# Hybrid attention trunk on one core: value products five steps behind the scores, inverse sums of two heads turned together

## The reference, cut to what matters

```python
logits = jnp.einsum('bqhd,bkhd->bhqk', qb, k, preferred_element_type=jnp.float32) * scale
...
p = jax.nn.softmax(logits, axis=-1)
return jnp.einsum('bhqk,bkhd->bqhd', p.astype(v.dtype), v)
```

## Time and profile before

| | us |
|---|---|
| median of 3 runs | 3393.14 (3392.2 to 3406.85) |
| profiled execution, its own time | 3396.07 |
| its span | 3394.3 |
| PE, DVE, ACT, POOL busy | 3024.3, 1362.0, 880.8, 936.2 |
| granted clock of TensorE, mean | 0.94 |
| even attention | 290 to 684 |
| odd attention | 1963 to 2459: small kinds to 2283, then sel and win |

### The profile page before, as it was taken

The page is one execution under the profiler, slowest core; times in us unless marked ns, Lnnn a source line. Parts: engine busy times, 40 slices in busy tenths (PEclk is TensorE's granted clock), DMA queues, the critical chain, the costliest instruction groups (busy, mean ns, idle before and its releaser), DMA issues.

```text
span 3394.3 us, 38000 instructions
## 1 busy us (share of the span) xinstructions
PE 3024.3 (89%) x14116; PEld 2484.8 (73%) x14116; DVE 1362.0 (40%) x1945; ACT 880.8 (26%) x1593; POOL 936.2 (28%) x562
## 2 busy tenths in 40 slices
PE   8896778798999999999999966767689999999999
PEld 5775777775888888876788855656667888888867
DVE  4634666606222222227523246576534222222264
ACT  2204555513011011024200044545531111111131
POOL 2330033242233233252233202121132333333342
PEclk9998999999999999999999965769889999999999
DMA  4236321120111111111235252434311111111102
GB/s 158 107 118 174 94 72 42 32 99 25 50 50 43 49 49 43 50 58 43 80 148 195 78 142 71 97 79 102 87 58 44 47 47 49 45 48 49 61 33 75
DMA packets 73794, 253.72 MB, mean 75 GB/s; under 512 B 9699, under 2 KB 13283, under 8 KB 73367
## 3 DMA queue, kind: packets, MB, share of 16 engines
q1 hardware_dynamic: 58728, 196.35, 19.5%
q10 hardware_dynamic: 14944, 55.74, 4.2%
HBM read 203.99 MB, written 52.78 MB: 76 GB/s over the span
## 4 chain that ended last, share of the span: by engine, by line
PE 75%; DVE 15%; issue 4%; ACT 3%; DMA 1%; POOL 0%; SPq 0%; DVEq 0%; ACTq 0%; POOLq 0%
PE ACC L1033 59%; PE OP L1196 5%; PE ACC L1165 3%; PE OP L1212 3%; DVE PT L1791 3%; PE TR L1179 2%; DVE R L1641 2%; DVE T L1664 1%; DVE H L1667 1%; PE OP L1089 1%; DVE XL L1647 1%; ACT PT L1437 1%; DVE XF L1832 1%; DVE T L1689 1%; DVE HL L1692 1%
## 5 line engine op out<-in xcount | busy, mean ns | idle before, releaser
L863 POOL CAST WH<-RAW 128x1024 fp32r<-128x1024 f32 x203 | 216.3, 1066 | 1577.8 <-PE ACC L1033 1558.0
L1033 PE MATMUL ACC<-XH,WH 128*128 128x512 f32 x1792 | 575.4, 402 | 70.5 <-DVE XL L1647 39.0
L1033 PE MATMUL ACC<-XL,WH 128*128 128x512 f32 x1792 | 556.7, 392 | 0.0
L1033 PE MATMUL ACC<-XH,WL 128*128 128x512 f32 x1792 | 555.7, 391 | 0.0
L865 POOL TENSOR_TENSOR WL<-RAW,WH 128x1024 fp32r<-128x1024 f32 x203 | 495.6, 2442 | 24.2
L1033 PEld LDWEIGHTS ACC<-XH,WH 128*128 128x128 f32 x1792 | 337.6, 190 | 171.3 <-issue 87.7
L1033 PEld LDWEIGHTS ACC<-XL,WH 128*128 128x128 f32 x1792 | 339.3, 189 | 71.8
L1033 PEld LDWEIGHTS ACC<-XH,WL 128*128 128x128 f32 x1792 | 339.0, 189 | 71.9
L1394 ACT ACTIVATE HH<-T 128x1024 fp32r<-128x1024 f32 x64 | 67.9, 1061 | 1168.4 <-DVE T L1689 1168.4
L1696 DVE TENSOR_TENSOR M<-M,ACC 128x1024 f32<-128x1024 f32 x128 | 156.3, 1221 | 495.8 <-PE ACC L1033 495.8
L1033 PE MATMUL ACC<-HH,WH 128*128 128x512 f32 x1024 | 316.7, 390 | 17.0 <-DVE HL L1692 17.0
(11 more groups left out here) (193 smaller groups left out, 3636.7 us busy)
## 6 DMA issues: line engine op xcount, KB each, us to landing
RAW<-in_w SPq DMA_DIRECT2D x203, 512.0 KB, 3.4
QK<-y_odds SPq DMA_DIRECT2D x128, 256.0 KB, 5.0
y_odds<-HALVES ACTq DMA_DIRECT2D x16, 1024.0 KB, 5.0
QK<-y_foxs SPq DMA_DIRECT2D x48, 256.0 KB, 5.4
y_foxs<-HALVES ACTq DMA_DIRECT2D x8, 1024.0 KB, 5.1
y_kv<-Q ACTq DMA_DIRECT2D x8, 512.0 KB, 2.6
BIAS<-y_f SPq DMA_DIRECT2D x8, 512.0 KB, 7.0
H<-in_xT ACTq DMA_DIRECT2D x8, 512.0 KB, 6.9
```

Source lines behind the costliest of these rows:

```text
L863: nc.gpsimd.tensor_copy(WH[:, slot], RAW[:, slot]).then_inc(s_whi, 1)
L1033: mm = nc.tensor.matmul(acc[:, h * HALF:(h + 1) * HALF], w(k), x[:, k, h * HALF:(h + 1) * HALF], start=first and k == k0 and w is ws and x ...
```

## The change

`VALUE_LAG` goes from 3 to 5, and PE issues `values` ahead of `turn` in a step. The outputs follow at lag 6 in place of 4. PB has four buffers for large kinds in place of three, and OP's two banks alternate by half.

`norm` goes. For halves of head e = 1 alone POOL's `spread` lays the inverse sums of both heads, 64 columns a head, over a SPREAD buffer (in dilated jobs the sums into one, the minima into the other); three steps later PE's `turn_spread` turns its four blocks into the next TR buffer, and one step after that DVE multiplies the 128 rows of both heads in one instruction (in dilated jobs ACT copies the sums, DVE the minima, 128 rows each). That group's TR buffer is free at `s_fin` (sums: `s_dl`). The halves of the mla heads are split in eight pieces of 512 columns over steps 0 to 5. RV, SPREAD and PB have other places in memory.

```diff
-TURN_LAG, VALUE_LAG = 2, 3
+TURN_LAG, VALUE_LAG = 2, 5
+SPLIT_STEPS = {0: (0, 1), 1: (2,), 2: (3,), 3: (4, 5), 4: (6,), 5: (7,)}
...
-        depth = 8 if t.small else 3
+        depth = 8 if t.small else 4
...
+            if st.norm and st.norm.e == 1:
+                st.norm.groups = [group(0, 4, st.norm, what)
+                                  for what in (("sums", "minima") if st.norm.job.kind in DILATED else ("inverse",))]
...
             if g.seq > 2:
                 x = pt_groups[g.seq - 3]
-                if x.kind == "A":
-                    eng.wait_ge(s_ptD, x.d)
+                if x.what == "sums":
+                    eng.wait_ge(s_dl, x.half.dl)
+                elif x.half:
+                    eng.wait_ge(s_fin, x.half.fin)
                 else:
-                    eng.wait_ge(s_ptA, x.a)
+                    eng.wait_ge(s_ptD, x.tr)
...
+                def spread(h):
+                    wide = lambda x: x.rearrange("p (e x) -> p x e", e=2)[:, 4 * h.h:4 * h.h + 4].unsqueeze(3)\
+                        .to_broadcast([P, 4, 2, HD])
+                    parts = (RL,) if h.job.kind not in DILATED else (L, NM)
+                    for m, src in enumerate(parts):
+                        no = h.spread - len(parts) + m + 1
+                        if m == 0 and len(parts) == 1:
+                            pool.wait_ge(s_rl, h.rl)
+                        elif m == 0:
+                            pool.wait_ge(s_exp, h.tasks[-1].no + 1)
+                        wait(pool, s_nrm, no - 2)
+                        nc.gpsimd.tensor_copy(SPREAD[no % 2][:].rearrange("p (t e f) -> p t e f", t=4, e=2), wide(src))\
+                            .then_inc(s_spread, 1)
...
-                    if st.turn:
-                        split_turned(st.turn)
-                        if st.turn.i % 4 == 3 and st.turn.kind in DILATED:
-                            spread_sums(st.turn.half)
+                    if st.turn and st.turn.i % 4 == 3 and st.turn.e == 1:
+                        spread(st.turn.half)
...
-                        wait(pe, s_o, c.half.no)
+                        wait(pe, s_o, c.half.no - 1)
...
-                def norm(h):
-                    pe.wait_ge(s_rl, h.rl)
-                    wait(pe, s_o, h.no)
-                    wait(pe, s_cor, h.cor_before)
-                    for m, t in enumerate(h.tasks):
-                        if h.job.kind in DILATED:
-                            rows = PTF[:, h.no % 2, m * P:(m + 1) * P]
-                        else:
-                            rows = RL[:, t.col:t.col + 1].to_broadcast([P, P])
-                        mm = nc.tensor.matmul(OP[:, 1, m * P:(m + 1) * P], rows, IDENT[:], start=True, stop=True)
-                    mm.then_inc(s_nrm, 1)
+                def turn_spread(h):
+                    for m, g in enumerate(h.groups):
+                        no = h.spread - len(h.groups) + m + 1
+                        pe.wait_ge(s_spread, no)
+                        group_free(pe, g)
+                        for b in range(4):
+                            tr = nc.tensor.transpose(TR[:, g.ring, b * P:(b + 1) * P],
+                                                     SPREAD[no % 2][:, b * P:(b + 1) * P], IDENT[:])
+                        tr.then_inc(s_nrm, 1)
...
+                    if st.values:
+                        values(st.values)
                     if st.turn:
                         turn(st.turn)
-                    if st.values:
-                        values(st.values)
                     if st.norm:
-                        norm(st.norm)
+                        turn_spread(st.norm)
...
-                    V_.tensor_tensor(dst, OP[rows, 0], CORR[rows], ALU.add).then_inc(s_o1, 1)
-                    dve.wait_ge(s_o1, h.o1)
-                    dve.wait_ge(s_nrm, h.no + 1)
-                    V_.tensor_tensor(dst, dst, OP[rows, 1], ALU.mult).then_inc(s_o, 1)
+                    V_.tensor_tensor(dst, OP[rows, h.no % 2], CORR[rows], ALU.add).then_inc(s_o, 1)
+                    if h.groups:
+                        x = O[:, cols] if j.kind in ("sel", "win") else XF[:, j.chunk, cols]
+                        dve.wait_ge(s_o, h.no + 1)
+                        dve.wait_ge(s_nrm, h.spread)
+                        V_.tensor_tensor(x, x, TR[:, h.groups[0].ring], ALU.mult).then_inc(s_fin, 1)
```

More of the change, by code:

```diff
@@ L320, in build_attention, with group @@
         t.acc_free = max(t.no - depth + 1, run0)
-        depth = 8 if t.small else 3
-        t.pb = t.no % depth
+        depth = 8 if t.small else 4
+        t.pb = t.no % depth if t.small else (t.no + 2) % depth
         t.pb_free = max(t.no - depth + 1, run0) - 1
-    count = dict(seq=0, a=0, d=0, b=0)
+        if not t.small and t.no < run0 + 2:
+            t.pb_free = -1
+    count = dict(seq=0, a=0)
     groups = []
-    def group(first, size, kind):
+    def group(first, size, half=None, what=None):
         count["seq"] += 1
-        count["a"] += 1
-        count["d" if kind == "A" else "b"] += 1
-        groups.append(Group(count["seq"], first, size, kind, count["a"], count["d"], count["b"]))
+        count["a"] += half is None
+        groups.append(Group(count["seq"], first, size, count["a"], half, what))
         return groups[-1]
@@ L359, in build_attention @@
                 if target and target.kind == "mla":
-                    st.split = (target, 1 - e, st.logits.i - 2)
+                    st.split = (target, 1 - e, SPLIT_STEPS[st.logits.i])
             if st.start and st.start.kind != "cmp":
-                st.start.vgroups = [group(g, 4, "A") for g in range(2)]
+                st.start.vgroups = [group(g, 4) for g in range(2)]
             if st.turn:
                 for g0 in range(0, len(st.turn.blocks), 4):
-                    kind = "A"
-                    st.turn.groups.append(group(g0, min(4, len(st.turn.blocks) - g0), kind))
-                st.turn.turned = count["seq"]
+                    st.turn.groups.append(group(g0, min(4, len(st.turn.blocks) - g0)))
+                st.turn.turned = count["a"]
+            if st.norm and st.norm.e == 1:
+                st.norm.groups = [group(0, 4, st.norm, what)
+                                  for what in (("sums", "minima") if st.norm.job.kind in DILATED else ("inverse",))]
             ph.steps.append(st)
@@ L1774, in scores @@
                     wait(dve, s_tr, t.pb_turned)
-                    if t.i % 4 == 0:
-                        wait(dve, s_nrm, t.no // 4 - 3)
+                    before = t.job.before
+                    if t.i % 4 == 0 and t.e == 0 and before and before.kind in DILATED:
+                        dve.wait_ge(s_spread, before.halves[2 + t.i // 4].spread)
                     V_.tensor_tensor_reduce(prob(t)[:, 0:w], score_bank(t), bias(t),
@@ L1798, in inverse_sums @@
                     c0 = h.tasks[0].col
-                    gated = h.job.kind in NSA
                     r = RL[:, c0:c0 + 4]
                     dve.wait_ge(s_exp, h.tasks[-1].no + 1)
+                    before = h.job.before
+                    if before and before.kind not in DILATED:
+                        dve.wait_ge(s_spread, before.halves[2 + h.h].spread)
                     V_.reciprocal(r, L[:, c0:c0 + 4]).then_inc(s_rl, 1)
-                    if gated:
+                    if h.job.kind in NSA:
                         dve.wait_ge(s_rl, h.rl - 1)
```

134 lines of the change are left out of this document (55 added, 79 removed).

## The result

The changed kernel takes 3223.9 us (median of 4 runs, 3220.1 to 3224.5), the kernel before 3396.2 on the same chip: a ratio of 0.9486, 95% interval 0.9461 to 0.951. The gain is 172 us where 116 were forecast; the forecast, 3277 us, missed by 53 and its range ended 1 us above the result. The direction was right, and every stage gave at least something; the sizes were not.

The account below looks back on a forecast made before the run. PE, busy for 89% of the span, was taken as the bound, its attention idleness mostly waits for DVE. Even -40, sel and win -21, dilated -50, merges -5: -116 on 3396.1, 3280, median 3 lower: 3277 us; range 3225 to 3340.

Parts of the forecast that it names:

- rival 1: The wait only moves: value products' 21.3, 11.7 and 44.9 us return in full ahead of turns; 3338 us; chance 0.17.
- Products of inverse sums: Turns replace eight-pass products on PE: 22.6 us less in even stage, 11.3 in sel/win, 21.3 in dilated jobs.
- I add 2 us a head ..., my choice and not a reading: Even attention: 16 x 2 us allowed for steps where DVE or ACT has more to do than PE.
- I keep the clock: Granted clock stays: 0.92 in even stage, sel/win too, 0.61 and 0.70 in dilated stretches; counted at 0 us.
- Rival 2: Higher clock: 24 us in dilated jobs, 20 in even and sel/win, 3233 us; sign above 0.9 dilated; chance 0.13.
- Dilated jobs: Two dilated stretches: 24 halves at 6.6 us in place of 8.7, 50 us less, near 26 us a job.
- In cmp DVE sets the pace, so I count nothing there: Cmp jobs: DVE sets the pace, so dropping PE's products of inverse sums there was counted at nothing.
- merges -5: Two merges: DVE loses four multiplications of 0.69 us, in 99 us with DVE busy for 85.7; 5 us less.
- Sel and win: Sel and win stage: 11.3 us less from products and 10 less waiting, 21 us less in all.
- Rival 3: 52 spread groups hold turn buffers, 2.9 us each: 3428 us; decides from 2.2 us a group; chance 0.05.
- Rival 4: Lower clock: even stage and sel/win fall from 0.92 to 0.63 or so, 3377 us; chance 0.05.
- At nothing: Counted at no cost: POOL's 52 spreads, finer MLA split, fourth PB buffer, two more steps at a stage's end.

Follow-up runs that it names:

- run 1: Changed kernel with value products back at three steps behind the scores and behind the turn, spread inverse sums kept: 3309.2 us, ratio 0.9758.
- run 4: Changed kernel with the score products of the cmp jobs issued twice: 3231.0 us, ratio 0.9518.
- run 12: Changed kernel with VALUE_LAG = 3 alone, value products still ahead of the turn: 3407.6 us, ratio 1.0039.
- run 2: Kernel before with VALUE_LAG = 5 and values ahead of turn, eight-pass products of inverse sums kept: 3297.1 us, ratio 0.9715.
- run 8: Changed kernel with the coarse split of the MLA heads as before, whole rows at steps 2 to 5: 3223.5 us, ratio 0.9498.
- Run 11: Changed kernel with one value bank, and OP's second bank used as a third turn buffer: 3183.2 us, ratio 0.9377.
- run 10: Changed kernel with the value products of all halves in one PSUM bank: 3244.9 us, ratio 0.9557.
- run 5: Changed kernel with the four transpositions of each spread group issued twice: 3239.0 us, ratio 0.9541.

## Why the prediction was wrong

*What bounds the kernel, and where the waits go:* right. The value products' waits, 21 us in the even stage, are 0.0; nothing of them came back ahead of turns there (28 us in place of 36). In the small jobs rival 1 had a good part of it: of 67 us ahead of value products, some 42 came back ahead of turned probabilities (48 in place of 6). As a forecast of the whole, at 3338 us, it is out.

*Products of inverse sums:* right for the even stage (28 of less work against 22.6) and sel and win (15 against 11), 15 against 21 in the dilated jobs. The 96 spread turns there were not cheaper than forecast; the work that they replace was counted at the chain's 1.83 us a half, where PE's share was 1.79, so a remainder of 6 us stays unexplained, near what the estimate can tell.

*"I add 2 us a head ..., my choice and not a reading":* the first step that failed. The three waits at a job's start, walked at 3.6 us a job, 29 in all, came true: 1.3 + 1.1 + 1.5 = 3.9 us at each of the seven starts, and 29 with the stage's end. The allowance, 32 us, measured 17, 1.1 us a head: the 3.9 behind the multiplications in mid-job, 6.8 for ACT's exponential, 5.3 for subtractions, 1.1 of scores waiting for DVE's minimum. Waits in all are 46 us where 61 were forecast. That value products with an old operand cover more of DVE's long steps than I gave them is my reading of it, not shown by a run of its own.

*"I keep the clock":* the step that weighed most. By the estimate above, 28 us in the dilated jobs and 14 in the even stage are PE doing the same work faster; between run 1 and the change, which issue the same instructions, busy time fell by 23 and 18 us there. Rival 2 had the mechanism at 0.13 and sized it at 44 us; these 42 would have put the forecast at 3235. Its own sign, above 0.9 in the dilated jobs, did not come: 0.82 and 0.83. What made me set it aside were 40 us at 1.2 GHz with PE busy for 75% and 24 us at 2.4 GHz with 72%. The reading that busy share alone does not decide was right (run 4 and run 12 say so again); the conclusion that the clock therefore stays was not. That a stage moved between both levels within one kernel was evidence that it could move, and should have widened the range downwards. The result lies only 1 us below the range, and this step is more than enough to account for that.

*Dilated jobs:* 137 us for six, 22.8 each, where 26 were forecast; without the clock they would have been near 27.5.

*"In cmp DVE sets the pace, so I count nothing there", and merges -5:* the third step. 18 us in place of 5 (and the four multiplications that the 5 stands on are 4 x 0.69 = 2.8 us). DVE was busy for 39.0 and 40.9 of 48 and 50 us and is for 33.1 and 33.4 of 40 now, 83% beside 82: both fell together. These 13.4 us less of DVE are as much as the merge's two reciprocals of 3.35 us, which with the later outputs come two steps later, in both cmp jobs behind the first score of the next job. In the kernel before both stood inside; in the changed one they start right behind the cut, for the first cmp job so:

```profile
L1857 DVE RECIPROCAL DL<-DL 128x512 f32<-128x512 f32 x2 | 6.7, 3350 | 0.0
```

```profile
2003.92 3.35 DVE L1856 RECIPROCAL DL<-DL 128x512 f32<-128x512 f32 x1
...
2009.11 3.35 DVE L1856 RECIPROCAL DL<-DL 128x512 f32<-128x512 f32 x1
```

So part of the stage's 18 us is DVE's work moved beside the next job, where PE sets the pace, and the forecast had not counted that two steps of lag move the merge too. What it costs in the next job was not parted. In run 1 the reciprocals stay inside and cmp gains 7 us for both jobs; in run 2 they move and it gains 9. The other part of the step is PE's time. Ahead of value products of the cmp jobs PE waited for DVE 12 us a job:

```profile
L1196 PE MATMUL OP<-PT,VCS 64*128 64x256 f32 x32 | 12.1, 475 | 24.4 <-DVE PT L1791 24.4
```

Run 4 shows that PE's time is not free there: 6.4 us more of PE make the job 2.2 longer. How the 18 us divide between the two stays open.

*Sel and win:* 15 of 21; the idle time fell by 6 in place of 10, and the clock by 0.04, which run 8 shows to be within what this stage does by itself.

*Rival 3,* turn buffers as the bound: not slower, but its reading was the fruitful one. At a job's start groups cost 1.1 us and the turn behind them 1.5, together more than the 2.2 from which it would decide; in mid-job the two cost 0.5. Run 11 shows what a third buffer is worth: 62 us over run 10. *Rival 4:* out, the clock rose in the even stage (0.93 to 0.98); in sel and win it fell by the 0.04 above. *At nothing:* right for the split (run 8); PE never waited for POOL's spread.

In the end, with the estimates of the table, 116 + 42 (clock) + 14 (waits, even) + 5 (work, even) + 13 (cmp) is 190, less 6 + 5 in the dilated jobs and 6 in sel and win is 173.

## What to carry to other kernels

Before a consumer behind a loop through two other engines is moved ahead of the producer's step, give it an operand that is several steps old: order alone lost everything that age and order together gained. (Age alone was not run.) When a change closes gaps in a stage that runs between the two levels of the clock, carry the clock as a case with real weight, not as a footnote. And when a lag grows, follow all that hangs on it: here it carried 6.7 us of merge work a job from a stage that VectorE paced into one that it did not. A busy share of 85% on that engine was no proof that TensorE's time was free either; a third of what run 4 added came out as time.

## What was not expected of the hardware

Transpositions and products held the granted clock alike: 0.94 in sel and win and 1.00 in the even stage in both runs that double the passes. The Trainium skill, TensorE: Matmul & The Clock Gate, Part 4 (PE-mode transpose), says that work in transpose mode does not count as busy time of the engine in the same way as products. No run here bears it out, though all these stages hold products beside the transpositions and none holds transpositions alone.

The clock did not follow PE's busy share: 0.50 in run 4's cmp job at 69%, 0.58 in run 5's at 56% (23.48 of 42 us), 0.82 in the changed kernel's d jobs at 84% (54.62 of 65 us), 0.64 in run 1's at 78% (65.86 of 84), 0.95 in run 12's even jobs at 74%. What does decide it is left open.
